# Two blocks in one kernel: a step's filling tile cut in two, 16 of its 24 matmuls ahead of the softmax transposes

## What is computed

```python
h = rmsnorm(x, attn_norm_g[l])
proj = jnp.einsum('bsd,de->bse', h, w_in[l])
gla_q, gla_k, gla_v, gla_r, gla_lr, mb_q, mb_k, mb_v, mem_q = jnp.split(proj, split_at, axis=-1)
...
o_gla = gla_chunked(...)                       # gated linear attention, 4 heads
o_moba = merge_heads(moba_attention(q_b, k_b, v_b, slopes))   # causal softmax with ALiBi, 4 heads
o_mem = merge_heads(memory_attention(q_c, k_c, split_heads(mem_v, MEM_HEADS)))  # softmax over 256 memory tokens
mix = jnp.concatenate([o_gla, o_moba, o_mem], axis=-1)
x = x + jnp.einsum('bse,ed->bsd', mix, w_out[l])
x = x + hierarchical_moe(rmsnorm(x, ffn_norm_g[l]), ...)
```

## Time and profile before

| | |
|---|---|
| time, median of 3 runs | 1773.83 us (1771.87 to 1775.69) |
| the profiled execution | 1772.83 us |
| its span from first to last instruction | 1771.0 us, 19920 instructions |
| TensorE busy | 1700.7 us (96%), 8096 matmuls |
| VectorE, ScalarE, GpSimd busy | 704.8, 607.5, 578.2 us |
| mean granted TensorE clock | 0.986 |
| the 16 pairs with their filling tiles | from about 45 to 216 us of the span |

### The profile page before, as it was taken

One profiled execution on the slowest core, in us unless ns is written; L12 is line 12 of the kernel. 1 busy time (PEld: TensorE's weight loads), 2 busy tenths in 40 slices (PEclk: granted clock), 3 DMA queues, 4 the chain that ended last, 5 costly groups with the idle time before them and its releaser, 6 DMA issues.

```text
span 1771.0 us, 19920 instructions
## 1 busy us (share of the span) xinstructions
PE 1700.7 (96%) x8096; PEld 1177.5 (66%) x8096; DVE 704.8 (40%) x1107; ACT 607.5 (34%) x787; POOL 578.2 (33%) x279
## 2 busy tenths in 40 slices
PE   7989799999999999999999989999999999999996
PEld 5667575444444444437788867777778788888885
DVE  6564744333433343348651023333344421212146
ACT  5564444111011101114751245554333432323232
POOL 3232134221022102014344435554443444434341
PEclk9999999999999999999999999999999999999999
DMA  5121164799999999983212111112242123232301
GB/s 207 60 74 43 42 269 144 296 420 421 421 421 421 421 421 421 420 348 119 80 64 95 48 48 48 48 48 91 82 161 95 63 103 118 86 105 95 115 28 48
DMA packets 79067, 312.73 MB, mean 177 GB/s; under 512 B 3168, under 2 KB 6656, under 8 KB 54272
## 3 DMA queue, kind: packets, MB, share of 16 engines
q1 hardware_dynamic: 78704, 310.38, 45.0%
q0 software_dynamic: 272, 1.05, 0.2%
HBM read 307.22 MB, written 4.19 MB: 176 GB/s over the span
## 4 chain that ended last, share of the span: by engine, by line
PE 86%; DVE 8%; ACT 3%; issue 1%; POOL 1%; DMA 0%; DVEq 0%; SPq 0%; ACTq 0%
PE ps L888 43%; PE ps L1242 13%; PE ps L936 7%; PE ps L1266 6%; PE ps L1195 4%; PE ps L886 2%; PE ps L1385 2%; PE ps L1211 1%; PE ps L1212 1%; PE ps L1374 1%; ACT sb_slot L1468 1%; PE ps L1422 1%; PE ps L1359 1%; DVE sb_xT L2283 1%; DVE sb_h_low L2004 1%
## 5 line engine op out<-in xcount | busy, mean ns | idle before, releaser
L827 POOL TENSOR_TENSOR sb_w_parts<-sb_slot,sb_w_parts 128x2048 fp32r<-128x2048 f32 x59 | 274.8, 4658 | 387.9 <-ACT sb_w_parts L1468 387.9
L888 PE MATMUL ps<-sb_h_high,sb_w_parts 128*128 128x512 f32 x1120 | 270.2, 393 | 2.5 <-POOL sb_w_parts L827 2.5
L888 PEld LDWEIGHTS ps<-sb_h_high,sb_w_parts 128*128 128x128 f32 x1120 | 210.3, 188 | 50.9 <-POOL sb_w_parts L827 3.4
L1468 ACT ACTIVATE sb_w_parts<-sb_slot 128x2048 fp32r<-128x2048 f32 x59 | 112.7, 1912 | 195.7 <-PE ps L888 186.7
L1242 PE MATMUL ps<-sb_slot,sb_hT 128*64 128x512 f32 x768 | 171.1, 594 | 0.0
L888 PE MATMUL ps<-sb_hidden_high,sb_w_parts 128*128 128x512 f32 x704 | 166.8, 392 | 1.9 <-ACT sb_hidden_high L1468 1.9
L888 PEld LDWEIGHTS ps<-sb_hidden_high,sb_w_parts 128*128 128x128 f32 x704 | 133.2, 189 | 30.1 <-ACT sb_hidden_high L1468 2.3
L791 POOL TENSOR_TENSOR sb_tile_parts<-sb_slot,sb_tile_parts 128x1024 fp32r<-128x1024 f32 x32 | 79.6, 2489 | 201.3 <-ACT sb_tile_parts L1468 201.3
L888 PE MATMUL ps<-sb_h_low,sb_w_parts 128*128 128x512 f32 x560 | 138.6, 390 | 0.0
L1242 PEld LDWEIGHTS ps<-sb_slot,sb_hT 128*64 128x64 f32 x768 | 53.6, 137 | 106.2 <-issue 106.2
L813 POOL TENSOR_SCALAR sb_chosen<-sb_cst,sb_small 128x256 fp32r<-128x256 f32 x28 | 25.3, 921 | 293.5 <-PE ps L1195 293.5
(11 more groups left out here) (325 smaller groups left out, 2644.7 us busy)
## 6 DMA issues: line engine op xcount, KB each, us to landing
sb_slot<-w_up SPq DMA_DIRECT2D x24, 2048.0 KB, 14.5
sb_slot<-w_gate SPq DMA_DIRECT2D x24, 2048.0 KB, 14.4
sb_slot<-w_down SPq DMA_DIRECT2D x21, 2048.0 KB, 15.4
sb_slot<-w_in SPq DMA_DIRECT2D x14, 2048.0 KB, 7.9
sb_R<-w_down SPq DMA_DIRECT2D x11, 2048.0 KB, 15.1
sb_slot<-tiles SPq DMA_DIRECT2D x32, 512.0 KB, 3.3
sb_R<-w_gate SPq DMA_DIRECT2D x8, 2048.0 KB, 14.2
sb_R<-w_up SPq DMA_DIRECT2D x8, 2048.0 KB, 14.9
```

The costliest lines, as they stand in the source:

```text
L827: nc.gpsimd.tensor_tensor(low, raw_part(g), high.bitcast(F32), ALU.subtract).then_inc(w_low, 1)
L888: ins = nc.tensor.matmul(o, w[:, k, at:at + P], h[:, k, :], start=first, stop=last)
L1468: return nc.scalar.activation(dst, src, f, **kw)
```

## The change

A new kind of step, `passes`, stands between the scores and the transposes of steps 1 to 9 and 11 to 14. It issues the first 16 matmuls of the step's first filling tile, with the wait for its bank. Where the tile itself stood, behind the values, its last 8 matmuls are left. Jobs keep their numbers, and so their banks; the other engines pass over the new step.

```diff
@@ -132,6 +132,8 @@
                 jobs.append(("score", i, hh))
             step("score", i)
         if 1 <= i <= len(PAIRS):
+            if i < len(PAIRS) and fills[i][0] != "gla_out":
+                step("passes", *fills[i][0])
             for hh in range(2):
                 job("turn", i - 1, hh)
         if i >= 2:
@@ -965,10 +967,15 @@
-            pending = []
+            pending, begun = [], set()
             for st in steps:
                 kind, arg = st[0], st[1:]
-                if kind == "tile":
+                if kind == "passes":
+                    tile(*arg, range(KD), True, True, ((0, 0), (1, 0)))
+                    begun.add(arg)
+                elif kind == "tile" and arg in begun:
+                    tile(*arg, range(KD), True, True, ((0, 1),))
+                elif kind == "tile":
                     if arg[0] == "out":
                         out_tile(arg[1])
```

## The result

The changed kernel takes 1787.6 us (median of 4 executions, 1786.1 to 1789.3), the kernel before 1774.8 us beside it (4 executions, 1771.9 to 1776.3). The ratio is 1.008, with a 95% interval from 1.0068 to 1.0092: slower by 12.8 us, where 1786 was forecast. The profiled execution has a span of 1784.3 us, 13.3 more than before.

The account below looks back on a forecast made before the run. TensorE, busy 96% of the span, was taken to bound the kernel. 7.5 us of waits removed and 19.3 new gave +11.8, plus 1.5 for the clock: +13.3, forecast 1786 us, range 1776 to 1798.

Parts of the forecast that it names:

- the walk: TensorE's waits after the change, step by step from 2 to the last pair: 27.1 us against 15.3, +11.8 us.
- Two signs: If right, tile r2 starts at about 236 us (223.35 before) and ScalarE's exponentials no longer wait for the maxima.
- the four waits for POOL: Second tiles of pairs 2 to 5: TensorE waits 0.8 to 1.0 us for low weights, four times.
- The transposes: Softmax transposes waiting for normalized probabilities: 3.84 us more matmuls ahead of them remove 7.5 us of waits.
- The bank: A tile's first matmul waits for a PSUM bank freed late; in step 13 free at T + 5.3, TensorE at T + 4.3.
- the change closes a loop: Passes, transposes, ScalarE, VectorE, bank, passes: step 13 can't be shorter than 9.1 us, against TensorE's own 8.1 us.
- The subtraction that took 2.89 us: VectorE's L2144, steps 3 and 5: taken as 0.7 us without POOL beside it; at 2.89 the sum is 3 us higher.
- The clock: Slow-clock events behind waits, each costing nothing to 1.5 us: -1.5 to +6 us in all, taken as +1.5.
- The event at step 4: Low clock, 0.66, right behind the wait at 92.30 us: the one of three events said to go.
- Faster: Rival: banks are free when TensorE comes, so 7.5 us of waits and three clock events go: 1762 us, chance 0.07.
- One wait for another: Rival: ScalarE and VectorE chain bounds both kernels, TensorE only waits at another place: 1771 to 1777 us, chance 0.09.
- Slower by more: Rival: waits in nearly every step each cost 1.5 us of clock, L2144 long: 1794 us and up, chance 0.17.

Follow-up runs that it names:

- the free bank: Changed kernel, with the first filling tiles of steps 8 and 14 in a spare PSUM bank, number 7: 1785.0 us, ratio 1.0065.
- the early eviction: Changed kernel, with VectorE evicting a step's first filling tile ahead of scaling the probabilities, from step 1 on: 1781.2 us, ratio 1.0036.
- the order with the 16 behind the transposes: Changed kernel, with the first 16 matmuls of the filling tile issued after the transposes and ahead of the values: 1785.9 us, ratio 1.0073.
- early-split kernel: Changed kernel, with ScalarE splitting the next tile's weights ahead of copying the transposes: 1786.1 us, ratio 1.0071.
- both together: Changed kernel, with the next weight tile split ahead of the transposes' copy and the eviction ahead of the scaling: 1781.7 us, ratio 1.0043.
- the moba pairs alone: Changed kernel, with the new step only in steps 1 to 7, the others as in the kernel before: 1777.8 us, ratio 1.0024.
- the cut in steps 4 and 6: Tile cut, with its eviction ahead of the scaling, in these two steps only, the others as before: 1778.2 us, ratio 1.0029.
- the eviction first on the kernel before: Kernel before, with only the eviction of a step's first filling tile moved ahead of the scaling on VectorE: 1774.8 us, ratio 1.0014.

## Why the prediction was right, point by point

**The size.** Forecast +13, measured +12.8. By parts, in the stretch: the waits gave +10.8 instead of +11.8 (27.9 against 17.1 us with L991 and its former line L984 in both sums, L1131 and its former line's 4.6 us in neither). The remaining 4.4 us of the stretch's 15.2 are 1.2 us for the thirds on their own (13 x 0.09) and, by difference, some 3 us of low clock. About 1 us came back behind the stretch, and the stretch began 1 us earlier.

That the total fits to within 1 us is in part luck. In the rows that the walk priced, the waits grew by 8.8 us and not by 11.8 (24.1 against 15.3, by their unrounded lengths). What made up for it was not in the sum: 2.0 us at L991 and 1.2 us for the cut thirds, and 1.5 us more of low clock, less the 2 us named just above. Two signs that the prediction named fit less well than the total: the first matmul of tile r2 started at 239.1 us, where 236 was forecast, and ScalarE's waits for the maxima are halved and not gone (20.8 us in 6 pairs, 42.6 in 12 before). They are gone in the mem pairs with a tile and stay in four moba pairs, so there the exponentials still waited for the maxima, which the prediction had named as a sign of being wrong.

**The walk.** Apart from step 1, which it didn't price, it held step by step to within 1 us: the bank 2.73 us at step 8 (forecast 3.1), 0.9 at step 9 (1.1), 0.5 and 2.0 at step 10 (0.65, 2.1), 1.4, 0.8 and 0.8 at step 13 (1.4, 1.0, 0.9), 2.3 at step 14 (2.65), 1.6 and 2.6 at step 15 and the last pair (1.8, 2.8); step 2 1.5 (2.5), step 7 3.05 (2.25); the four waits for POOL 0.8 each (0.8 to 1.0).

**The transposes.** Right: their 7.5 us are gone.

**The bank.** The chain was right, and the wait is real: the free bank took away the two waits that it was meant for, and the early eviction those for L1977. But "the change closes a loop: passes, transposes, ScalarE, VectorE, bank, passes" names as the cause what is only the place where it shows. Without passes ahead of the transposes the loss in time was the same 12.7 us, though only half of the added waits were there. The link that both orders share is ScalarE's copy of the values, behind 16 matmuls and in front of split and exponentials; the prediction has the copy in its list, but closes the loop over the transposes. By that loop the order with the 16 behind the transposes should have been near the kernel before, and I expected it there. That the values' copy is the link that decides is the best reading of the runs, and is not shown by one that takes it out.

**What lengthens the loop.** The subtraction that took 2.89 us beside POOL takes 0.69 in the kernel after, where POOL is elsewhere, and 2.70 in the early-split kernel, where POOL is back. The Trainium skill (SBUF — State Buffer, section "Who interferes with whom") says that a VectorE instruction with two SBUF inputs contends with a POOL instruction that reads SBUF, and this trace agrees; by that rule the prediction took 11.8 us for its sum and not 15. The scaling beside POOL took its forecast time too: 1.46 us in steps 13 and 14 of the kernel after, 0.62 alone.

**What was not in the sum.** Step 1 waits 3.8 us at L991 (1.84 before). The split of the next tile moved behind a later copy, so POOL worked from 57.73 to 60.46 us beside VectorE's addition L1933, which took 3.36 us where it took 1.2. It is the same effect as the one just named, at a place where I didn't look for it, and worth 2.0 us. The 0.1 us per cut third is the second.

**The clock.** I took +1.5 within a range of -1.5 to +6 (by its own terms, with one of the events gone, the upper end is +4.5); it was about +3 in the stretch, so this term was mis-sized by half. The event at step 4 went, as said. Those behind the waits of steps 2 and 7 grew: their 16 matmuls take 6.16 and 6.35 us where they took 5.06 and 4.61, in part because they now stand right behind the wait, where the slow transposes and values stood before. A new one follows the 2.0 us at step 10: the gated output's groups take 1.22 us instead of 0.71, and the next 16 matmuls 5.81. The 2.73 us at step 8 had none behind it. In return the 16 matmuls of the tile behind the last pair take 4.32 us, 5.80 before. In these traces a wait's length doesn't tell whether an event follows.

**The rivals.** "Faster" needed ScalarE's chain to be 1 us shorter. The early split takes the 1.05 us of the weight split out from between copies and exponentials, and was no faster than the kernel before (1786.1 us), with VectorE slowed by POOL at other places. The order on VectorE that spoke against it was the right objection: turning it round gave half of the loss back, but no gain over the kernel before. "One wait for another" is nearly true in steps 0 to 7 (+2.7 us, 2.0 of them at L991) and not in the mem pairs (+12.6). "Slower by more" would have shown between 138 and 160 us; the clock stayed at 1.00 there.

## What to carry to other kernels

Before work is put in front of a product, look at what every engine has queued behind that product's copy: here ScalarE's exponentials stood behind the copies of transposes and values, and VectorE's scaling behind the exponentials, so a matmul in front of the values delayed a softmax that has nothing to do with them. In a ring of in-order engines a wait that is removed is worth only what the next one in the ring allows; a wait list of one kernel doesn't price another's steps. A walk along the ring came close for this change, but the theory that went with it missed its range for most of the variants, so a total that fits doesn't prove the mechanism. And to find the cause, vary the amount and the place apart: 0, 8 and 16 matmuls gave 0, +4.3 and +12.8 us, and the place relative to the transposes changed which waits there were and left the time as it was.

## What the runs showed of the hardware that was not expected

A group of 8 matmuls of 512 columns takes 0.1 us longer when it is issued apart from the 16 of the same tile (2.12 against 2.03 us at full clock).

Between 345 and 365 us (DMA busy for the whole window) and between 790 and 810 us the clock stayed at 1.00 in the kernel before and after, but stood at 0.91 in the profiles of the early split, the eviction first, both together and the moba pairs alone, and between 0.94 and 0.99 in two more (the cut in steps 4 and 6, and the eviction first on the kernel before). From the output tiles to the end the first three and the cut in steps 4 and 6 took 3.6 to 5.3 us longer than the kernel before (1533.8 us), the other two did not. Nothing of the change is there. What sets it off is open.
